# Rotary embedding in an attention layer: exchanging the two halves with VectorE's shuffle instead of a TensorE product

## The reference

```python
def apply_rope(x, cos, sin):
    xf = x.astype(jnp.float32)
    half = xf.shape[-1] // 2
    x1, x2 = xf[..., :half], xf[..., half:]
    return jnp.concatenate([x1 * cos - x2 * sin, x2 * cos + x1 * sin], axis=-1).astype(x.dtype)
...
for l in range(DEPTH):
    h = rms_norm(x, pre_norm[l])
    proj = h @ w_in[l]
    (dq, dk, dv, dgate, gq, gk, gv, ggate, mq, mgate) = jnp.split(proj, IN_OFFSETS, axis=-1)
    dq = apply_rope(dq ..., *lin_cs)      # 6 heads x 2 parts of 32 channels
    dk = apply_rope(dk ..., *lin_cs)
    ...
    gq = rms_norm(gq ..., gqa_q_norm[l])  # 6 heads of 64, as 2 x 32 for rows and columns
    gq = apply_axial_rope(gq, row_cs, col_cs)
    gk = rms_norm(gk ..., gqa_k_norm[l])
    gk = apply_axial_rope(gk, row_cs, col_cs)
    ...
    y = jnp.concatenate([oa, ob, om], axis=-1) @ w_out[l]
    x = x + rms_norm(y, post_norm[l])
```

## Time and profile before

| | |
|---|---|
| median of 3 runs | 2799.99 us (2799.65 to 2803.03) |
| the profiled execution: its span, and the only time the profile gives for it | 2801.1 us |
| PE busy | 2699.8 us (96%) |
| DVE busy | 1442.6 us (51%) |
| ACT busy | 1099.5 us (39%) |
| POOL busy | 697.3 us (25%) |
| mean granted TensorE clock | 0.985 of full speed |

### The profile page before, as it was taken

One profiled execution on the slowest core, in us unless ns is written; L12 is line 12 of the kernel. 1 busy time (PEld: TensorE's weight loads), 2 busy tenths in 40 slices (PEclk: granted clock), 3 DMA queues, 4 the chain that ended last, 5 costly groups with the idle time before them and its releaser, 6 DMA issues.

```text
span 2801.1 us, 35940 instructions
## 1 busy us (share of the span) xinstructions
PE 2699.8 (96%) x13734; PEld 2219.0 (79%) x13734; DVE 1442.6 (51%) x1988; ACT 1099.5 (39%) x1787; POOL 697.3 (25%) x601
## 2 busy tenths in 40 slices
PE   6998999999999999999999999999999998999998
PEld 6875688766788888888798888887888886988887
DVE  5566655664475442587364442465432774644423
ACT  3357643376443422423352222342222475422222
POOL 1037430165368700245020000156000200200000
PEclk9999999999999999999999999999999999999999
DMA  3320023200144423444222323345223443232232
GB/s 128 120 76 1 16 69 117 73 31 1 46 92 134 145 77 97 134 136 143 96 76 91 103 76 93 102 165 217 90 83 99 157 149 99 76 101 93 76 94 71
DMA packets 307740, 269.26 MB, mean 96 GB/s; under 512 B 44595, under 2 KB 297948, under 8 KB 304028
## 3 DMA queue, kind: packets, MB, share of 16 engines
q1 hardware_dynamic: 300780, 241.71, 27.9%
q0 software_dynamic: 2800, 20.25, 1.8%
q10 hardware_dynamic: 4032, 5.57, 0.7%
HBM read 239.74 MB, written 27.77 MB: 95 GB/s over the span
## 4 chain that ended last, share of the span: by engine, by line
PE 75%; DVE 7%; POOL 5%; issue 3%; ACT 3%; POOLq 2%; DVEq 2%; SPq 1%; DMA 1%; ACTq 0%
PE bank L421 22%; PE bank L422 22%; PE bank L423 22%; POOL E L1830 2%; POOLq L1829 2%; PE bank L1992 2%; PE bank L1318 2%; DVE XL L481 1%; ACT WH L383 1%; POOL MBB L796 1%; POOL MBA L796 1%; DVE X L585 1%; DVE work L581 1%; DVE WL L388 1%; PE bank L1978 1%
## 5 line engine op out<-in xcount | busy, mean ns | idle before, releaser
L421 PE MATMUL bank<-XH,WH 128*128 128x512 f32 (+1 forms) x2400 | 901.5, 376 | 36.2 <-DVE WL L388 13.6
L422 PE MATMUL bank<-XL,WH 128*128 128x512 f32 (+1 forms) x2400 | 890.9, 371 | 0.0
L423 PE MATMUL bank<-XH,WL 128*128 128x512 f32 (+1 forms) x2400 | 889.3, 371 | 0.0
L388 DVE TENSOR_TENSOR WL<-raw,WH 128x2048 fp32r<-128x2048 f32 (+1 forms) x208 | 443.6, 2133 | 537.2 <-ACT WH L383 536.9
L421 PEld LDWEIGHTS bank<-XH,WH 128*128 128x128 f32 x2400 | 456.1, 190 | 133.5 <-DVE WL L388 18.9
L383 ACT ACTIVATE WH<-raw 128x2048 fp32r<-128x2048 f32 (+1 forms) x208 | 362.5, 1743 | 460.2 <-PE bank L423 459.7
L422 PEld LDWEIGHTS bank<-XL,WH 128*128 128x128 f32 x2400 | 456.8, 190 | 84.6 <-issue 3.3
L423 PEld LDWEIGHTS bank<-XH,WL 128*128 128x128 f32 x2400 | 456.2, 190 | 81.8
L1115 POOL TENSOR_TENSOR ssq<-ssq,sq 128x512 f32<-128x512 f32 x24 | 30.9, 1289 | 1075.3 <-ACT sq L1024 1075.3
L422 PE MATMUL bank<-HL,WH 128*128 128x512 f32 (+1 forms) x792 | 293.9, 371 | 0.0
L423 PE MATMUL bank<-HH,WL 128*128 128x512 f32 (+1 forms) x792 | 293.4, 370 | 0.0
(11 more groups left out here) (410 smaller groups left out, 3643.3 us busy)
## 6 DMA issues: line engine op xcount, KB each, us to landing
raw<-in_ffn_w_dram SPq DMA_DIRECT2D x88, 1024.0 KB, 5.3
raw<-in_ffn_w_dram SPq DMA_DIRECT2D x64, 704.0 KB, 4.6
raw<-in_w_in_dram SPq DMA_DIRECT2D x24, 1024.0 KB, 5.2
MM<-mm_scr SPq DMA_DIRECT2D x12, 1152.0 KB, 7.4
raw<-in_w_out_dram SPq DMA_DIRECT2D x8, 1024.0 KB, 5.1
raw<-in_cv_w_in_dram SPq DMA_DIRECT2D x8, 1024.0 KB, 5.5
mm_scr<-MBA POOLq DMA_DIRECT2D x6, 1152.0 KB, 4.7
mm_scr<-MBB POOLq DMA_DIRECT2D x6, 1152.0 KB, 4.5
```

The costliest lines, as they stand in the source:

```text
L388: dve.tensor_tensor(WL[:, slot, 0:n * P], raw[:, slot, 0:n * P], WH[:, slot, 0:n * P].bitcast(F32), ALU.subtract).then_inc(l_done, 1)
L421: pe.matmul(out, WH[:, slot, c:c + P], h, start=start, stop=False)
L422: pe.matmul(out, WH[:, slot, c:c + P], l, start=False, stop=False)
L423: return pe.matmul(out, WL[:, slot, c:c + P], h, start=False, stop=stop)
```

## The change

The ten products by the permutation in each layer are gone from PE. `turn` now handles two tiles at once on DVE: two `stream_shuffle` from `PR` into `work1` with the list `i ^ 16`, which exchanges partitions inside every group of 32, then two products by the cosines, a drain, two products by the sines (now `work1` by `rope`, in place), a drain, and two additions. A drain is also ahead of the shuffles. The semaphores `gn` and `swapped` disappear, and the constant `perm` is half as large.

```diff
-    perm = np.zeros((P, 2, P), np.float32)
-    perm[p ^ 16, 0, p] = 1.0
-    perm[:, 1] = (p[:, None] // 64 == p[None, :] // 64)
+    perm = (p[:, None] // 64 == p[None, :] // 64).astype(np.float32)
...
-            pool.dma_start(perm[:, :, :], io["perm_c"]).then_inc(ss(s, "mem_in"), 16)
+            pool.dma_start(perm[:, :], io["perm_c"]).then_inc(ss(s, "mem_in"), 16)
...
-            def swap(n):
-
-                j = ROPED[n][0]
-                if j >= GQ:
-                    pe.wait_ge(ss(s, "gn"), at(s, "gn", j - GQ + 1))
-                if n >= 2:
-                    pe.wait_ge(ss(s, "roped"), at(s, "roped", n - 1))
-                pe.matmul(bank[6 + n % 2][:, :], perm[:, 0, :], PR[:, j, :], start=True, stop=True)\
-                  .then_inc(ss(s, "swapped"), 1)
...
-            swap(0)
-            swap(1)
             block(5)
-            swap(2)
-            swap(3)
...
-            swap(4)
-            swap(5)
...
-            block(8, lambda: (swap(6), swap(7)))
+            block(8)
             value_turn(3)
-            block(9, lambda: (swap(8), swap(9)))
+            block(9)
...
-            def turn(n):
-
-                j, tab = ROPED[n]
-                if n == 0:
+            def turn(n0):
+
+                two = [(PR[:, ROPED[n][0], :], work1[:, n % 2, :], ROPED[n][1]) for n in (n0, n0 + 1)]
+                if n0 == 0:
                     dve.wait_ge(ss(s, "rope_in"), at(s, "rope_in", 16))
-                dve.wait_ge(ss(s, "swapped"), at(s, "swapped", n + 1))
-                dve.tensor_tensor(PR[:, j, :], PR[:, j, :], rope[:, tab, :], ALU.mult)
-                dve.tensor_tensor(work1[:, n % 2, :], bank[6 + n % 2][:, :], rope[:, tab + 1, :], ALU.mult)
                 dve.drain()
-                dve.tensor_tensor(PR[:, j, :], PR[:, j, :], work1[:, n % 2, :], ALU.add).then_inc(ss(s, "roped"), 1)
+                for x, other, _ in two:
+                    dve.stream_shuffle(other, x, [i ^ 16 for i in range(32)])
+                for x, _, tab in two:
+                    dve.tensor_tensor(x, x, rope[:, tab, :], ALU.mult)
+                dve.drain()
+                for _, other, tab in two:
+                    dve.tensor_tensor(other, other, rope[:, tab + 1, :], ALU.mult)
+                dve.drain()
+                for x, other, _ in two:
+                    dve.tensor_tensor(x, x, other, ALU.add).then_inc(ss(s, "roped"), 1)
```

More of the change, by code:

```diff
@@ L220, in program @@
         rb = ExitStack()
-        perm = sb("perm", [P, 2, P], F32, rb)
+        perm = sb("perm", [P, P], F32, rb)
         rb2 = ExitStack()
@@ L347, in program @@
             "attn": dict(mem_in=32, rope_in=16, mem_n=2, ml=KD, mem_t=KD, mh=KD, mrms=1, msq=2, vm_t=1, vmh=1, vml=1,
-                         v_t=4, vh=4, vl=4, gsq=4, gms=4, gln=4, grms=4, gn=4, swapped=10, roped=10, ready=1, gate=8,
+                         v_t=4, vh=4, vl=4, gsq=4, gms=4, gln=4, grms=4, roped=10, ready=1, gate=8,
                          s=91, e=91, nb=64, p=24, pn=40, rsum=64, scaled=24, qh=14, ql=14, pt=64, pt_a=52, pt_d=12, pv=32, o=16, osq=3, orms=3, og=3,
@@ L1858, in head_squares @@
                     pe.wait_ge(ss(s, "gln"), at(s, "gln", n))
-                pe.matmul(bank[5][:, :], perm[:, 1, :], ms_buf(n), start=True, stop=True)\
+                pe.matmul(bank[5][:, :], perm[:, :], ms_buf(n), start=True, stop=True)\
                   .then_inc(ss(s, "gms"), 1)
@@ L1958, in output_norms @@
                     pe.wait_ge(ss(s, "e"), at(s, "e", m - 3))
-                    pe.matmul(bank[m % 4][:, :], perm[:, 1, :], norm_buf(n), start=True, stop=True)\
+                    pe.matmul(bank[m % 4][:, :], perm[:, :], norm_buf(n), start=True, stop=True)\
                       .then_inc(ss(s, "s"), 1)
@@ L2291, in head_norm @@
                 g = headg[:, (2 if n < 3 else 4) + l:(3 if n < 3 else 5) + l]
-                dve.scalar_tensor_tensor(PR[:, GQ + n, :], PR[:, GQ + n, :], g, ms_buf(n), ALU.mult, ALU.mult)\
-                   .then_inc(ss(s, "gn"), 1)
-            def turn(n):
-                j, tab = ROPED[n]
-                if n == 0:
+                dve.scalar_tensor_tensor(PR[:, GQ + n, :], PR[:, GQ + n, :], g, ms_buf(n), ALU.mult, ALU.mult)
+            def turn(n0):
+                two = [(PR[:, ROPED[n][0], :], work1[:, n % 2, :], ROPED[n][1]) for n in (n0, n0 + 1)]
+                if n0 == 0:
                     dve.wait_ge(ss(s, "rope_in"), at(s, "rope_in", 16))
-                dve.wait_ge(ss(s, "swapped"), at(s, "swapped", n + 1))
-                dve.tensor_tensor(PR[:, j, :], PR[:, j, :], rope[:, tab, :], ALU.mult)
-                dve.tensor_tensor(work1[:, n % 2, :], bank[6 + n % 2][:, :], rope[:, tab + 1, :], ALU.mult)
                 dve.drain()
-                dve.tensor_tensor(PR[:, j, :], PR[:, j, :], work1[:, n % 2, :], ALU.add).then_inc(ss(s, "roped"), 1)
+                for x, other, _ in two:
[8 more added lines that the diff above has]
+                    dve.tensor_tensor(x, x, other, ALU.add).then_inc(ss(s, "roped"), 1)
             if s == stages[0]:
@@ L2310, in attn_dve @@
             turn(0)
-            turn(1)
             evict(5)
@@ L2314, in attn_dve @@
             turn(2)
-            turn(3)
             evict(6)
@@ L2318, in attn_dve @@
             turn(4)
-            turn(5)
             evict(7)
@@ L2324, in attn_dve @@
             turn(6)
-            turn(7)
             evict(8)
@@ L2328, in attn_dve @@
             turn(8)
-            turn(9)
             evict(9)
```

## The result

| | before | after |
|---|---|---|
| median | 2799.82 us (2797.64 to 2803.03, 4 runs) | 2781.66 us (2780.26 to 2784.36, 4 runs) |
| the profiled execution: span | 2801.1 us | 2778.5 us |
| PE, DVE, POOL busy | 2699.8, 1442.6, 697.3 us | 2677.9, 1457.0, 688.8 us |

The ratio is 0.9933, 95% interval [0.9922, 0.9944]: 18.2 us faster. The forecast was 2780.8 us (ratio 0.9931), range 2778.5 to 2788.5. The median of before was 2799.8 to 2801.3 us from one set of runs to another, so an experiment is compared with the changed kernel best by its ratio to the before measured beside it.

What follows compares the result with a forecast made beforehand. PE, busy 96% of 2801.1 us, was taken as the bound. Its 19.5 us saved, less 0.3 for a late `ready`, made 19.2 off the median of 2800.0: 2780.8 us, range 2778.5 to 2788.5.

Steps and rivals of the forecast that it cites:

- PE sets the pace: In `attn0` between block boundaries PE is busy throughout, except 13.89 of 14.49 us in block 8; DVE waits for it.
- What PE gets back: Per layer, four pairs of products at 1.72 us and block 8's at 2.86: 9.74 us, 19.5 for two layers.
- The price of a shuffle: On DVE, no earlier trace had one: taken as 0.70 us, near a copy of the same shape, 1.75 for the range.
- The tight place: DVE from head norms to `ready`: margin 0.1 us, so shuffles at 0.70 make `ready` 0.3 us late.
- The cover of the first three pairs: After blocks 4, 5 and 6, DVE's 4.54 us idle covers 1.4 us more per pair; fails above 2 us a shuffle.
- Slack of 1.1 us in `attn1`, none in `attn0`: Between POOL's first sum of probabilities and PE's transposes: late `ready` paid in full in `attn0`, after 1.1 us in `attn1`.
- POOL in the way: Rival, chance 0.14: POOL's instruction near 164 slows additions of turn(6), up to 1.3 us more; gain 17.9, time 2782.1.
- The prediction's own rule: Lateness of `ready` costs its full size in `attn0` and 1.1 us less in `attn1`.
- the dearer shuffles among the prediction's rivals: DVE becomes the bound, chance 0.13: shuffles of 1.34 us give 2785.2, 1.75 give 2788.4; slower than before, 0.03, from 3.2.
- a bound from above: Upper limit for a shuffle's price on DVE: an SBUF copy of 64 x 512 took 1.34 us beside POOL.

## Why the prediction was right, point by point

**PE sets the pace.** Right. PE is busy for the whole of blocks 5, 8, 9 and 10, and the products put back without any wait restore 17.0 of the 18.2 us (16.8 by the ratios).

**What PE gets back.** 9.71 us against 9.74 in `attn0`; block 8 gave 2.86 and block 9 1.71, as worked out. The two halves of the change, measured apart, gave 10.3 and 8.6 where the steps had 10.3 and 9.2. The time itself, 2781.66 us for a forecast of 2780.8, lies within what three measurements of the gain differ by (16.6 to 19.8), so it tells nothing finer than the rows do.

**The price of a shuffle.** I took 0.70 us and measured 0.65 from one to the next; the record itself is 0.745. The guess was on the careful side of a row of the same shape. The cost of the record of 14 ns ahead of each shuffle (`LOAD_MASK_SELECT`) lies within the 0.65. The Trainium skill (VectorE: DVE Perf Modes, The perf-mode tier table) led to an estimate of 0.60, scaled in proportion to the elements; the trace is 8% above it.

**The tight place.** Right as to where, and the margin was as thin as worked out: ACT's split ended at 172.51 + 1.92 = 174.43, and `low_w(13)` started at 174.58, 0.15 us later, where before's lag was 0.03 (181.82 + 1.92 = 183.74, and 183.77). So the change made `ready` 0.12 us late; forecast 0.3, and with the shuffle at 0.65 the working itself gives 4 x 0.05 - 0.1 = 0.1. ACT waited 0.11 us longer. The kernels with extra shuffles show how much the place decides: 17.5 us of shuffles cost nothing a few blocks earlier, 11.7 us here cost 16.1.

**The cover of the first three pairs.** Right that it holds, wrong in size. The working took before's wait of 4.54 us as the room for a dearer pair, but PE itself now comes 1.72 us earlier: 4.54 - 1.72 - 1.5 is the 1.31 us that is left. A second wait of 1.31 us, ahead of `low_w`, was not counted. The early extra shuffles used up both, 2.9 us a pair, at no cost in time, so by this estimate a shuffle of 0.65 + 2.9 / 2 = 2.1 us would still have been covered there. Where the cover ends was not measured.

**Slack of 1.1 us in `attn1`, none in `attn0`.** Right in size; the place was read a step too late. In the changed kernel POOL's sum ends at 559.13 + 1.30 = 560.43 and PE transposes at 561.42, 1.0 us of slack; in `attn0` it is 198.25 and 198.34. But in neither kernel does PE wait at these transposes. It had already waited, in `attn0` alone, at the two scores that need the banks of the first exponentials: 0.67 us before (201.72 to 203.63, against the 1.24 us without a wait) and 0.79 with the change. POOL's sum hangs on the same exponentials, so that a late `ready` is paid in full either way, and sending it earlier moved the transposes of `attn0` alone.

**POOL in the way.** The mechanism was there, and that it cost nothing was luck by a few tenths of a us. L2285, two inputs from SBUF, took 2.35 us for two at 128.15 instead of 1.27 while POOL worked on its low part. That is in turn(2), with cover. In turn(6), where it would have counted, POOL's instruction started at 164.36, as near 164 as the prediction had it, and the two additions ran from 163.36 in 1.29 us:

```profile
164.36 1.45 POOL L1818 TENSOR_TENSOR PRr<-PR,PRr 128x512 fp32r<-128x512 f32 x1 [6.33 <-ACT PRr L2094]
```

They touched only for the last 0.3 us, and it was POOL's that grew a little (1.45 us for 1.29). In `attn1` it was the same (528.24 us, 1.45). The late extra shuffles, which moved DVE by 3 us, did meet it (2.23). The Trainium skill (SBUF — State Buffer, Who interferes with whom) says that a VectorE instruction with two SBUF inputs and a GpSimd one that reads SBUF exclude each other, and one with a single input outside the two-port modes doesn't contend; the traces agree with both: the shuffles at 140.22 and 140.87 took 0.75 and 0.74 us beside POOL's instruction of 139.44 to 141.25, as elsewhere.

```profile
139.44 1.81 POOL L1818 TENSOR_TENSOR PRr<-PR,PRr 128x512 fp32r<-128x512 f32 x1 [9.49 <-ACT PRr L2094]
```

```profile
140.22 0.75 DVE L2283 STREAM_SHUFFLE work<-PR 128x512 f32<-128x512 f32 x1
```

The Trainium skill says in the same section that copies can take a two-port mode and then contend; 0.42 us alone and 1.34 or 1.42 beside POOL agree.

**What was wrong** besides was a step for an experiment, not for the change: in the expectation for the late shuffles I added up durations from undisturbed rows and came to 10.5 us. Moving work on DVE by several us changes what it lies beside. The prediction's own rule, fed with the lateness that the trace shows, gives 14.5. The same holds for the prices of the dearer shuffles among the prediction's rivals: a lateness of several us also reaches PE through `low_w(13)` and the evictions of block 10, which their sums leave out.

## What to carry to other kernels

Price an operation taken from the bounding engine by the length of the window around it, not by the record of the operation: the pair of products inside block 8 was worth 2.86 us, with the wait ahead of it, and the other pairs 1.72. For the engine that takes over the work, look not at its busy share but for the one chain in which it has no wait left; here 17.5 us of extra work cost nothing ahead of it, and 11.7 us inside it cost 16.1. When work is shifted, recheck which two-input instructions now lie beside GpSimd's.

## What the runs showed of the hardware

- A VectorE shuffle of 128 x 512 float32 takes 0.745 us, with 14 ns for its list and 0.65 us from one to the next, a little more than a copy's 0.60, and is not slowed beside GpSimd's element-wise work (0.75 and 0.74 us).
- The same copy of 64 x 512 takes 0.42 us alone and 1.34 to 1.42 beside GpSimd's element-wise work, over three times as long. The 1.34 us that the prediction took as a bound from above is the price of the neighbour, not of the copy.
- Two-input instructions from SBUF go from 1.27 or 1.29 to 2.23 or 2.35 us for two beside one instruction of GpSimd; the split of 128 x 2048 from 2.28 to 2.74 and 3.07. The split grew where GpSimd's instruction had started first (174.28 against 174.99, 181.36 against 181.74 us) and kept its 2.28 where it was the first itself (174.58 against 175.02).
- One execution of before ran a fully busy stretch of 25 us at a mean granted clock of 0.87, where an execution of the changed kernel had 1.00. Comparing these two single traces, that stretch is worth about 3 us and must be taken off first.
